# A two-block transformer kernel: each weight chunk's upper and lower part placed at one of sixteen offsets inside its buffer

## The chip, the cores and the metric

The kernel runs on one core of one Trainium2 chip. The metric is the device time of one execution in microseconds (us), the median of several runs. TensorE (PE in the profile) does the matrix products, VectorE (DVE), ScalarE (ACT) and GpSimd (POOL) the rest, and SyncE (SP) issues the loads of the weights.

## The reference

The reference is two model blocks of two layers each, at 256 tokens and a width of 1024. The first has a feed-forward part, a token mixer of three kinds of heads and a second feed-forward part in every layer; the second has a mixer of three other kinds and a feed-forward part with a convolution. Nearly all the arithmetic is in products of the tokens with large weight matrices:

```python
y = swiglu(modulate(x, ...), ffn_w13[l, 0], ffn_w2[l, 0])       # 1024 -> 2*2816 -> 1024
x = layer_norm(ALPHA * x + 0.5 * (1 + mod[:, 0, 2])[:, None, :] * y, ...)
y = token_mixer(modulate(x, ...), w_in[l], w_out[l], ...)
...
proj = x @ w_in                                                  # 1024 -> 4608, second block
u = depthwise_conv_centred(x @ w_up, conv_w, conv_b)             # 1024 -> 2*2816
ffn = (jax.nn.silu(gate) * val) @ w_down
```

## The kernel before

The weights come in 369 chunks of at most 128 partitions by 2048 float32 (8192 bytes a partition, 1 MB in all) in an order fixed beforehand (`SCHED`). 295 of them are matrices (`MATS`), numbered m from 0; the others feed a small sum on VectorE and play no part here. SyncE loads a chunk into one of four buffers `W`. ScalarE copies it, rounded to the reduced float32 of the PE array, into one of three buffers `H` (the upper part, line 586). VectorE subtracts that copy from `W` and writes the remainder into one of three buffers `L` (the lower part, line 601). Chunk m uses `H[m % 3]` and `L[m % 3]`. The tokens are held split in the same way (`XH` and `XL`, `hh` and `hl`, `mixh` and `mixl`, and `eh` and `el` for the first stage), and each product is made of three: upper by upper, lower by upper, upper by lower.

TensorE takes chunk m in one of these ways, each matmul with its own load of the stationary operand of 128 columns:

- `up` (lines 713 to 715): the stationary operand is a 128-column slice of `H` or `L`, the moving operand is 256 columns of `XH` or `XL`. In a chunk there are 2 tiles of 8 rows of 3 matmuls.
- `tokens` (742 to 744): the other way round, the stationary operand is of `XH` or `XL` and the moving one is 256 columns of `H` or `L`. In the first stage `eh` and `el` stand for `XH` and `XL` in both.
- `opening` (729 to 732): as `up`, in another order, for the first chunk of a stage.
- `down_bank` (757 to 759): the stationary operand is of `hh`/`hl` (feed-forward) or `mixh`/`mixl` (mixers), the moving one is 512 columns of `H` or `L`.

The order of the work is written out by program and is the same on every run. Semaphores tie it: ScalarE may write `H[m % 3]` when TensorE has done chunk m - 3 (`released`), VectorE waits for ScalarE, TensorE waits for VectorE (`lo_done`), and SyncE refills a `W` buffer when VectorE has read it.

Where the buffers lie follows from their sizes and the order in which they are allocated. In bytes of a partition: `H` at 68256, 76448 and 84640, `L` at 92832, 101024 and 109216, all of them 160 beyond a multiple of 512. `hh` and `hl` (117408, 139936), and `eh` and `el` (133792, 141984), are also 160 beyond a multiple of 512. `XH`, `XL`, `mixh` and `mixl` (from 200672 on) are 480 beyond one. Every slice that the matmuls take inside them starts a multiple of 512 bytes further on.

Of the kernel before, what the change touches and what calls it, by code (L numbers as in the profile page):

```python
# [9 lines left out]
F32R = mybir.dt.float32r  # L10
# [4 lines left out]
ADD, SUB, MUL, MAX, MIN = ALU.add, ALU.subtract, ALU.mult, ALU.max, ALU.min  # L15
# [7 lines left out]
CH = 2048  # L23
NW = 4
NH = 3
# [100 lines left out]
def width(c):  # L126
    return len(MIXCOLS[c[2]][1]) if c[0] == "win" else 256
# [189 lines left out]
def rr(ap, pattern, **k):  # L317
    return ap.rearrange(pattern, **k)
# [10 lines left out]
class Core:  # L329
# [22 lines left out]
    def keep(self, name, shape, dt=F32):  # L352
        t = self.place(name, shape, self.at, dt)
        self.at += self.size(shape)
        return t
# [11 lines left out]
    def buffers(self):  # L367
        keep = self.keep
        self.C = keep("cst", [128, NCONST])
        self.COL = keep("cols", [128, NROW])  # L370
        self.HD = keep("heads", [128, 4])
        self.CV = keep("cv", [128, 8])
        self.SC = keep("sc", [128, 8])
        self.POS = keep("pos", [128, 2], I32)
        self.CS = keep("cs", [128, 2, 2, 8])
        self.ones = keep("ones", [128, 128])
        self.AB = keep("ab", [128, 16])
        self.mod = [keep(f"mod{i}", [128, 3, 8]) for i in range(2)]
        self.X = keep("x", [128, 2, D])
        self.W = [keep(f"w{i}", [128, CH]) for i in range(NW)]  # L380
        self.H = [keep(f"h{i}", [128, CH], F32R) for i in range(NH)]
        self.L = [keep(f"l{i}", [128, CH], F32R) for i in range(NH)]
        x = self.top = self.top - 7 * 4096
        self.XH, self.XL = self.place("xh", [128, 8, T], x, F32R), self.place("xl", [128, 8, T], x + 8192, F32R)
        self.mixh1, self.mixl1 = self.place("mixh", [128, 8, T], x, F32R), self.place("mixl", [128, 8, T], x + 8192, F32R)
        g = self.gate_at = x + 16384
        self.G = self.place("gate", [128, D], g)
        self.acc = [self.place(f"acc{i}", [128, D], g + 4096 * i + 4096) for i in range(2)]
        self.GB2 = self.place("gb2", [128, 2, D], g + 4096)
        self.base = self.at  # L390
        self.ln_at = self.top - (8192 + 8192 + 2048 + 4096 + 128)
        ln = self.stack(self.ln_at, R=[128, 2, D], GB=[128, 2, D], tmp=[128, 2, 2, 128], tmp0=[128, 8, 128], st=[128, 2, 16])
        self.R, self.GB, self.tmp, self.tmp0, self.st = (ln[k] for k in ("R", "GB", "tmp", "tmp0", "st"))
        const = lambda k: self.C[:, CW[k][0]:CW[k][0] + CW[k][1]]
        self.ident, self.neg, self.causal, self.lvl, self.eye, self.both = (const(k) for k in ("ident", "neg", "causal", "lvl", "eye", "both"))
        self.ones64, self.rmask, self.freq, self.sgn, self.mhalf = (const(k) for k in ("ones64", "rmask", "freq", "sgn", "mhalf"))
        f = self.stack(self.base, hh=[128, NF, T], hl=[128, NF, T], sa=[128, 4, T], hf=[128, 2, T], yb=[128, 2, T])
        self.hh, self.hl, self.sa, self.hf, self.yb = (f[k] for k in ("hh", "hl", "sa", "hf", "yb"))
        assert f["end"] <= self.ln_at, (f["end"], self.ln_at)
        k = self.stack(self.base, memf=[128, 8, T], xf=[128, 8, T], eh=[128, 8, T], el=[128, 8, T], ftmp=[128, 8, T])  # L400
        self.memf, self.xf, self.eh, self.el, self.ftmp = (k[n] for n in ("memf", "xf", "eh", "el", "ftmp"))
        assert k["end"] <= self.ln_at
        k = self.stack(self.ln_at, mk0=[128, 4, T], mv0=[128, 2, 512], mk1=[128, 4, T], mv1=[128, 2, 512], z=[128, 2, 4, 8], p=[128, 2])
        self.kvb = [[k["mk0"], k["mv0"]], [k["mk1"], k["mv1"]]]
        self.rot_z, self.rot_p = k["z"], k["p"]
        assert k["end"] <= self.top
# [140 lines left out]

def made(m):  # L550

    return m + 2


class Feed:
# [5 lines left out]
    def load(self):  # L561
        k, e, n = self.k, self.e, self.n
        self.n += 1
        if n >= NW:
            o = n - NW
            if SCHED[o][0] == "ada":
                e.wait_ge(k.ada_sum, 2 * sum(c[0] == "ada" for c in SCHED[:o + 1]))
            else:
                e.wait_ge(k.lo_done, made(MATPOS.index(o)))
        z = 8 * width(SCHED[n])  # L570
        parts = [slice(0, 1024), slice(1024, CH)] if n == 0 else [slice(0, z)]
        for i, c in enumerate(parts):
            if n == 0:
                e.dma_start(k.memf[:, 4 * i:4 * i + 4, :], k.dram["memT"][:, 4 * i:4 * i + 4, :]).then_inc(k.d_mem[i], 16)
            e.dma_start(k.W[n % NW][:, c], k.dram["stream"][n][:, c]).then_inc(k.landed[n % NW] if n or i else k.d_first, 16)

    def hi(self, upto):

        k, e = self.k, self.e
        while self.m <= min(upto, len(MATS) - 1):  # L580
            m, n = self.m, MATPOS[self.m]
            z = 8 * width(MATS[m])
            e.wait_ge(k.landed[n % NW], 16 * (n // NW + 1))
            if m >= NH:
                e.wait_ge(*k.released(m - NH))
            e.copy(k.H[m % NH][:, 0:z], k.W[n % NW][:, 0:z]).then_inc(k.hi_done, 1)  # L586
            self.m += 1

    def lo(self, upto):

        k, e = self.k, self.e
        while self.n < len(SCHED) and (self.m <= upto or SCHED[self.n][0] == "ada"):
            n, c = self.n, SCHED[self.n]
            self.n += 1
            if c[0] == "ada":
                self.sum_ada(n, c)
                continue
            m, z = self.m, 8 * width(c)
            self.m += 1
            e.wait_ge(k.hi_done, made(m))  # L600
            e.tensor_tensor(k.L[m % NH][:, 0:z], k.W[n % NW][:, 0:z], k.H[m % NH][:, 0:z], SUB).then_inc(k.lo_done, 1)  # L601

    def sum_ada(self, n, c):
        k, e, v = self.k, self.e, self.a // 4
# [74 lines left out]
class Pe:  # L679
# [5 lines left out]
    def open(self):  # L685

        k, m = self.k, self.m
        self.m += 1
        self.p.wait_ge(k.lo_done, made(m) if m else 1)
        n = width(MATS[m])  # L690
        rows = 2 if MATS[m][0] in DOWN else 8
        v = lambda b: rr(b[:, 0:8 * n], "p (k n) -> p k n", k=rows)
        return v(k.H[m % NH]), v(k.L[m % NH])

    def bank(self):
        k, t = self.k, self.t
# [2700 lines left out]
```

## Time and profile before

| | |
|---|---|
| median of 3 runs | 2102.08 us (2100.36 to 2103.16) |
| span of the profiled execution | 2101.3 us |
| TensorE busy | 2002.5 us, 95% |
| weight loads of TensorE busy | 1854.1 us, 88% |
| VectorE busy | 1575.3 us, 75% |
| ScalarE busy | 1073.1 us, 51% |
| GpSimd busy | 308.4 us, 15% |
| granted TensorE clock, mean | 0.983 |

The profile gives the span of its execution, from the first to the last instruction, and no other time of it; the span is 0.8 us below the median of the runs. Matmuls are pipelined, so the duration of one (280 ns for one of 256 columns) is longer than the distance from its start to the next one's start. It is this distance, called the pace below, that times the work.

### The profile page before, as it was taken

The page shows a single profiled execution, that of the slowest core. Times are in us where ns is not written, and L with a number is a line of the kernel's source. Part 1 is how long each engine was busy: PE and PEld are TensorE (multiplying, and loading weights), DVE is VectorE, ACT ScalarE, POOL GpSimd, SP SyncE. Part 2 cuts the span into 40 slices and gives each one's busy share as a digit, 9 for nine tenths or more (in the row PEclk, how much of TensorE's full clock was granted, in tenths as well). Part 3 has the DMA queues.
Part 4 walks back from the last instruction along what each step waited for, and adds up shares of the span by engine and source line. Part 5 has one row for each costly group of instructions (what it writes and reads, how often), then busy time and mean ns, then how long its engine had stood idle before and what let it go on. Part 6 is the DMA issues. An engine that isn't in the chain of part 4 may idle for free.

```text
span 2101.3 us, 39270 instructions
## 1 busy us (share of the span) xinstructions
PE 2002.5 (95%) x16744; PEld 1854.1 (88%) x16744; DVE 1575.3 (75%) x2135; ACT 1073.1 (51%) x1516; POOL 308.4 (15%) x247
## 2 busy tenths in 40 slices
PE   7999989999999999899999999898999997989998
PEld 7999879979998998789889989887899887979996
DVE  6688788766987677688675649886788489758874
ACT  4543365455434443564554435565665375646652
POOL 0200032111000200203011004610120036002100
PEclk9999999999999999999999999899999999999999
DMA  9888743335985677443245663233465533324552
GB/s 378 325 315 330 279 161 132 106 120 203 354 340 205 243 284 303 148 163 122 82 173 207 252 226 118 101 141 115 147 202 193 205 125 141 122 101 161 202 199 80
DMA packets 60381, 409.85 MB, mean 195 GB/s; under 512 B 6896, under 2 KB 6896, under 8 KB 13872
## 3 DMA queue, kind: packets, MB, share of 16 engines
q1 hardware_dynamic: 54000, 384.85, 49.4%
q0 software_dynamic: 5920, 22.07, 3.1%
q8 instruction: 133, 2.18, 0.4%
q10 hardware_dynamic: 288, 0.42, 0.1%
q14 instruction: 40, 0.33, 0.0%
HBM read 404.17 MB, written 3.15 MB: 194 GB/s over the span
## 4 chain that ended last, share of the span: by engine, by line
PE 76%; DVE 14%; ACT 4%; POOL 2%; issue 2%; DMA 2%; SPq 0%; DVEq 0%; POOLq 0%; ACTq 0%
PE ps L713 13%; PE ps L714 13%; PE ps L715 13%; PE ps L757 7%; PE ps L759 6%; PE ps L758 6%; DVE l L601 4%; PE ps L742 2%; PE ps L1725 2%; PE ps L744 2%; PE ps L743 2%; DMA w<-in_stream 2%; PE ps L625 1%; DVE tmp L975 1%; ACT h L586 1%
## 5 line engine op out<-in xcount | busy, mean ns | idle before, releaser
L601 DVE TENSOR_TENSOR l<-w,h 128x2048 fp32r<-128x2048 f32 (+1 forms) x295 | 672.7, 2283 | 150.1 <-ACT h L586 149.7
L713 PE MATMUL ps<-xh,h 128*128 128x256 f32 x2544 | 722.3, 284 | 19.3 <-DVE gq L2423 9.4
L586 ACT CAST h<-w 128x2048 fp32r<-128x2048 f32 (+1 forms) x295 | 557.0, 1893 | 331.4 <-PE ps L759 162.1
L714 PE MATMUL ps<-xl,h 128*128 128x256 f32 x2544 | 713.6, 281 | 0.0
L715 PE MATMUL ps<-xh,l 128*128 128x256 f32 x2544 | 712.9, 280 | 0.0
L713 PEld LDWEIGHTS ps<-xh,h 128*128 128x128 f32 x2544 | 480.4, 189 | 27.6 <-DVE l L601 12.3
L714 PEld LDWEIGHTS ps<-xl,h 128*128 128x128 f32 x2544 | 480.3, 189 | 2.4 <-issue 2.4
L715 PEld LDWEIGHTS ps<-xh,l 128*128 128x128 f32 x2544 | 480.1, 189 | 0.0
L757 PE MATMUL ps<-h,hh 128*128 128x512 f32 x528 | 207.4, 393 | 0.0
L759 PE MATMUL ps<-h,hl 128*128 128x512 f32 x528 | 205.6, 389 | 0.0
L758 PE MATMUL ps<-l,hh 128*128 128x512 f32 x528 | 205.5, 389 | 0.0
L618 DVE SCALAR_TENSOR_TENSOR acc<-w,sc,acc 128x1024 f32<-128x1024 f32 x126 | 165.2, 1311 | 3.8 <-DMA w<-in_stream 1.1
L742 PE MATMUL ps<-h,xh 128*128 128x256 f32 (+1 forms) x512 | 150.8, 294 | 9.3 <-DVE l L601 9.3
L743 PE MATMUL ps<-l,xh 128*128 128x256 f32 (+1 forms) x512 | 145.6, 284 | 0.0
L744 PE MATMUL ps<-h,xl 128*128 128x256 f32 (+1 forms) x512 | 145.5, 284 | 0.0
L1021 POOL TENSOR_SCALAR st<-st 128x1 f32<-128x1 f32 x22 | 8.2, 374 | 814.8 <-DVE st L897 806.5
L759 PEld LDWEIGHTS ps<-h,hl 128*128 128x128 f32 x528 | 99.1, 188 | 20.8
L758 PEld LDWEIGHTS ps<-l,hh 128*128 128x128 f32 x528 | 99.2, 188 | 20.6 <-issue 0.5
L757 PEld LDWEIGHTS ps<-h,hh 128*128 128x128 f32 x528 | 99.1, 188 | 20.5 <-issue 0.5
L1254 DVE TENSOR_TENSOR hl<-hf,hh 128x256 fp32r<-128x256 f32 x132 | 55.6, 421 | 81.8 <-ACT hh L1249 81.1
L742 PEld LDWEIGHTS ps<-h,xh 128*128 128x128 f32 x512 | 100.1, 196 | 14.5 <-DVE l L601 10.3
L744 PEld LDWEIGHTS ps<-h,xl 128*128 128x128 f32 x512 | 100.3, 196 | 0.0
(425 smaller groups left out, 3007.1 us busy)
## 6 DMA issues: line engine op xcount, KB each, us to landing
w<-in_stream SPq DMA_DIRECT2D x361, 1024.0 KB, 4.9
GB<-in_vec POOLq DMA_DIRECT2D x20, 512.0 KB, 5.8
w<-in_stream SPq DMA_DIRECT2D x8, 512.0 KB, 4.1
gate<-in_vec POOLq DMA_DIRECT2D x6, 512.0 KB, 4.0
memf<-in_memT SPq DMA_DIRECT2D x2, 512.0 KB, 6.1
xf<-in_xT POOLq DMA_DIRECT2D x1, 1024.0 KB, 9.5
kv<-mk POOLq DMA_DIRECT2D x2, 512.0 KB, 6.1
kv<-mv POOLq DMA_DIRECT2D x2, 512.0 KB, 8.6
```

Of the source, the lines that this page charges most:

```text
L586: e.copy(k.H[m % NH][:, 0:z], k.W[n % NW][:, 0:z]).then_inc(k.hi_done, 1)
L601: e.tensor_tensor(k.L[m % NH][:, 0:z], k.W[n % NW][:, 0:z], k.H[m % NH][:, 0:z], SUB).then_inc(k.lo_done, 1)
L618: e.scalar_tensor_tensor(out=A[:, :], in0=W[:, i, :], scalar=k.SC[:, r:r + 1], in1=A[:, :], op0=MUL, op1=ADD).then_inc(k.ada_sum, 1)
L713: p.matmul(P[:, 0:T], H[:, r, o], xh[:, r, :], start=r == 0, stop=False)
L714: p.matmul(P[:, 0:T], H[:, r, o], xl[:, r, :], start=False, stop=False)
L715: i = p.matmul(P[:, 0:T], L[:, r, o], xh[:, r, :], start=False, stop=r == 7)
L742: p.matmul(P[:, 0:n], xh[:, r, o], H[:, r, :], start=r == 0, stop=False)
L743: p.matmul(P[:, 0:n], xh[:, r, o], L[:, r, :], start=False, stop=False)
L744: i = p.matmul(P[:, 0:n], xl[:, r, o], H[:, r, :], start=False, stop=r == 7)
L757: p.matmul(P[:, :], hh[:, f, o], H[:, i, s], start=b, stop=False)
L758: p.matmul(P[:, :], hh[:, f, o], L[:, i, s], start=False, stop=False)
L759: x = p.matmul(P[:, :], hl[:, f, o], H[:, i, s], start=False, stop=e)
```

## The change

`H` and `L` buffers grow by 128 elements (512 bytes a partition). A new function gives the place of chunk m: 8 elements (32 bytes) times m % 16 beyond the buffer's start. ScalarE's copy, VectorE's subtraction and TensorE's reads all use it.

```diff
-        self.H = [keep(f"h{i}", [128, CH], F32R) for i in range(NH)]
-        self.L = [keep(f"l{i}", [128, CH], F32R) for i in range(NH)]
+        self.H = [keep(f"h{i}", [128, CH + 128], F32R) for i in range(NH)]
+        self.L = [keep(f"l{i}", [128, CH + 128], F32R) for i in range(NH)]
...
+def place_in(b, m, z=CH, first=0):
+
+    o = 8 * (m % 16)
+    return b[m % NH][:, o + first:o + z]
...
-            e.copy(k.H[m % NH][:, 0:z], k.W[n % NW][:, 0:z]).then_inc(k.hi_done, 1)
+            e.copy(place_in(k.H, m, z), k.W[n % NW][:, 0:z]).then_inc(k.hi_done, 1)
...
-            e.tensor_tensor(k.L[m % NH][:, 0:z], k.W[n % NW][:, 0:z], k.H[m % NH][:, 0:z], SUB).then_inc(k.lo_done, 1)
+            e.tensor_tensor(place_in(k.L, m, z), k.W[n % NW][:, 0:z], place_in(k.H, m, z), SUB).then_inc(k.lo_done, 1)
...
-        v = lambda b: rr(b[:, 0:8 * n], "p (k n) -> p k n", k=rows)
-        return v(k.H[m % NH]), v(k.L[m % NH])
+        v = lambda b: rr(place_in(b, m, 8 * n), "p (k n) -> p k n", k=rows)
+        return v(k.H), v(k.L)
```

Chunk 0, which is written by two lines of its own, has the offset 0 in both kernels. No instruction is added, removed or moved on any of the five engines: the two programs are the same row by row, apart from addresses. `H` now starts at 68256, 76960 and 85664 and `L` at 94368, 103072 and 111776, still 160 beyond a multiple of 512, and chunk m lies 32 * (m % 16) bytes beyond that. What is allocated behind the six buffers (`hh`, `hl`, `eh`, `el` among it) moves up by 3072 bytes, which is a multiple of 512; `XH`, `XL`, `mixh` and `mixl` are counted from the top of the memory and stay.

## Rows read from the trace of the kernel before

**Rows 1.** The page: the span, and each engine's busy time.

```profile
span 2101.3 us, 39270 instructions
PE 2002.5 (95%) x16744; PEld 1854.1 (88%) x16744; DVE 1575.3 (75%) x2135; ACT 1073.1 (51%) x1516; POOL 308.4 (15%) x247
```

**Rows 2.** The page: the chain that ended last, shares by engine.

```profile
PE 76%; DVE 14%; ACT 4%; POOL 2%; issue 2%; DMA 2%; SPq 0%; DVEq 0%; POOLq 0%; ACTq 0%
```

**Rows 3.** Stretches of feed-forward work: busy us, granted clock, DMA share, GB/s.

```profile
680.00:800.00 120.00, 119.50 (x1004) 118.35 (x1004) 84.61 (x84) 54.83 (x65) 12.01 (x6) 1.00 0.71 268
1210.00:1270.00 60.00, 60.00 (x289) 50.36 (x288) 32.51 (x29) 16.89 (x9) 3.73 (x8) 1.00 0.58 208
```

**Rows 4.** Groups by form: busy us, mean ns; then idle time before.

```profile
L713 PE MATMUL ps<-xh,h 128*128 128x256 f32 x2544 | 722.3, 284 | 19.3 <-DVE gq L2423 9.4 <-DVE l L601 6.4 <-ACT K L3214 3.4
L601 DVE TENSOR_TENSOR l<-w,h 128x2048 fp32r<-128x2048 f32 x289 | 665.4, 2305 | 142.7 <-ACT h L586 142.5
L586 ACT CAST h<-w 128x2048 fp32r<-128x2048 f32 x289 | 550.7, 1910 | 321.8 <-PE ps L759 152.5 <-PE ps L715 77.7 <-DMA w<-in_stream 67.1
L757 PE MATMUL ps<-h,hh 128*128 128x512 f32 x528 | 207.4, 393 | 0.0
L742 PE MATMUL ps<-h,xh 128*128 128x256 f32 x480 | 141.8, 295 | 9.3 <-DVE l L601 9.3
L757 PE MATMUL ps<-h,mixh 128*128 128x512 f32 x160 | 69.4, 434 | 0.6
L729 PE MATMUL ps<-xh,h 128*128 128x256 f32 x144 | 41.8, 329 | 1.1 <-ACT mv L1091 0.7 <-DVE xl L1108 0.3
L713 PE MATMUL ps<-eh,h 128*128 128x256 f32 x64 | 19.5, 305 | 11.0 <-DVE l L1125 10.0 <-DVE l L601 0.9
```

**Rows 5.** Timeline, `up` in a feed-forward stage: start us, us; 51 starts apart.

```profile
699.86 0.28 PE L713 MATMUL ps<-xh,h 128*128 128x256 f32 x1
...
705.87 0.28 PE L713 MATMUL ps<-xh,h 128*128 128x256 f32 x1
```

**Rows 6.** Timeline, `up` late in the second mixer: 21 starts apart.

```profile
1428.66 0.28 PE L713 MATMUL ps<-xh,h 128*128 128x256 f32 x1
...
1431.04 0.28 PE L713 MATMUL ps<-xh,h 128*128 128x256 f32 x1
```

**Rows 7.** Timeline, `tokens` in the first stage: 42 starts apart.

```profile
61.52 0.28 PE L744 MATMUL ps<-h,el 128*128 128x256 f32 x1
...
66.56 0.28 PE L744 MATMUL ps<-h,el 128*128 128x256 f32 x1
```

**Rows 8.** Timeline, `tokens` in the second mixer: 39 starts apart.

```profile
1386.00 0.28 PE L742 MATMUL ps<-h,xh 128*128 128x256 f32 x1
...
1390.59 0.28 PE L742 MATMUL ps<-h,xh 128*128 128x256 f32 x1
```

**Rows 9.** Timeline, `down_bank` with `hh`: 96 starts apart.

```profile
1217.84 0.39 PE L757 MATMUL ps<-h,hh 128*128 128x512 f32 x1
...
1239.60 0.39 PE L757 MATMUL ps<-h,hh 128*128 128x512 f32 x1
```

**Rows 10.** Timeline, `down_bank` with `mixh`: 33 starts apart.

```profile
441.97 0.39 PE L757 MATMUL ps<-h,mixh 128*128 128x512 f32 x1
...
449.67 0.39 PE L757 MATMUL ps<-h,mixh 128*128 128x512 f32 x1
```

**Rows 11.** Waits, the largest of the weight chunks: us, times, longest us.

```profile
ACT h L586 <- PE ps L759: 162.1, 47, 5.5
DVE l L601 <- ACT h L586: 149.7, 74, 4.4
PE ps L742 <- DVE l L601: 12.4, 6, 3.6
```

## The prediction

> **What bounds the kernel now.** I read the page first. TensorE is busy for 2002.5 of the 2101.3 us [rows 1], and it holds 76% of the chain that ended last [rows 2]. Then I cut out stretches of the feed-forward stages with the view by windows. There TensorE has no gaps: 119.5 of 120 us and 60.0 of 60, at the full clock, while VectorE is busy for 84.6 of the 120 and the DMA engines are at 71% and 58% [rows 3]. The waits say the same from the other side. ScalarE waits 162 us in total for TensorE to give `H` back, and the costliest wait of TensorE for the lower part is 12.4 us [rows 11]. So the time of most stages is a count of matmuls times their pace, and the feeding engines have slack.
>
> The pace is what the change can touch, so I measured it in the timeline as the distance between two starts divided by their count. The reader should see that it isn't one number. I give it beside 106.7 and 213.3 ns, which are 256 and 512 columns at one per cycle of 2.4 GHz.
>
> - `up` in the feed-forward stages: 6.01 us for 51, so 117.8 ns [rows 5]. The same instruction late in the second mixer: 2.38 us for 21, so 113.3 ns [rows 6].
> - `tokens` with `eh`: 5.04 us for 42, so 120.0 ns [rows 7]. `tokens` with `xh`: 4.59 us for 39, so 117.7 ns [rows 8]; in most other places of the mixers its starts stand, by the timeline, as in [rows 6].
> - `down_bank` with `hh`: 21.76 us for 96, so 226.7 ns [rows 9]. With `mixh`: 7.70 us for 33, so 233.3 ns [rows 10].
>
> Two things follow. The same instruction with the same places relative to 512 bytes can run at 117.8 or 113.3 ns, so there are states that it falls into and keeps. And the partner counts: `eh` and `hh` lie 160 beyond a multiple of 512 like `H`, `xh` and `mixh` lie 480 beyond one, and with equal places 256 columns are slowest (120.0) while 512 columns are fastest (226.7). Apart from the addresses I find no difference between the `tokens` of [rows 7] and those of [rows 8]. That is an argument, not proof, that the relative place of the stationary and the moving operand sets part of the pace.
>
> **The change part by part.** No instruction is added, removed or moved. So every term is a count times a change of duration.
>
> ScalarE's copy and VectorE's subtraction: 1910 and 2305 ns [rows 4]. `W`, `H` and `L` all lie at 160 beyond a multiple of 512 today, which would be the worst case if their places could collide, and I take nothing from them and add nothing. If the copy grew by 5% (0.1 us of a chunk's 5.7 us, 48 matmuls by 117.8), the slack of the feeding engines would hide it [rows 3, 11]. The DMAs into `W` and their addresses don't change. The shift of the buffers behind by 3072 bytes keeps every place relative to 512. I cost both at nothing; TensorE's own work covers them, and bare they would be worth 0.1 us in a chunk.
>
> The matmuls: the relative place now goes through sixteen values, 32 bytes apart, one for each chunk. Only two of the sixteen relations (equal, and 320 bytes apart in one sense or the other) are seen in this trace, so each term is bounded by the lowest and the highest pace seen of the same shape: 113.3 to 120.0 ns for 256 columns and 226.7 to 233.3 for 512. The counts are three times those of [rows 4].
>
> - `up` with `xh`, 7632 at 117.8. The state was kept through whole stages while all chunks had one place. With a new place at each chunk I expect it to be drawn anew every 5.7 us. I take the lower state for half of the chunks and the middle of the two upper values, 118.9, for the other half: 116.1 ns, so 7632 x 1.7 = 13.0 us less. Bounds: 34 us less (all at 113.3) to 17 us more (all at 120.0).
> - `down_bank` with `hh`, 1584 at 226.7, the lowest seen. Half of the chunks at 233.3: 1584 x 3.3 = 5.3 us more. Bounds: 0 to 10.6 us more.
> - `tokens` with `xh` and `opening`, 1440 and 432, now between 113.3 and 117.8. From the middle, 115.6, to 116.1: 1.0 us more. Bounds: 4 us less to 8 us more.
> - `down_bank` with `mixh`, 480 at 233.3: half of the chunks at 226.7, 1.6 us less. Bounds: 3.2 us less to 0.
> - The first stage with `eh`, 384 at 120.0 to 116.1: 1.5 us less, of which some vanishes, since the stage also waits for its loads. Bounds: 2.6 us less to 0.
>
> Sum: -13.0 + 5.3 + 1.0 - 1.6 - 1.5 = -9.8 us. On the span of 2101.3 that gives 2091.5, and on the median, 0.8 us higher, 2092.3. I say 2092. The sum of the bounds is 44 us less to 36 us more, where all terms would have to end on one side.
>
> What a rule says against it: the Trainium skill (SBUF — State Buffer, Who interferes with whom) gives TensorE two independent read ports, one for the moving operand and one for the weights, and says that PE and ACT never wait on anyone. By it the sum would be zero and the time 2102. The rows above don't decide it, but 120.0 against 113.3 ns for the same shape is something that this rule alone doesn't explain.
>
> **The rivals.**
>
> *Places don't matter (2102).* The states come from how the queue of TensorE filled, and `eh` differs from `xh` by something else of its stage. For it: `up` has both 117.8 and 113.3 at the same places [rows 5, 6], so something other than the place sets at least that difference. Against it: 120.0 in the first stage and nowhere else, 226.7 with `hh` and 233.3 with `mixh` [rows 7, 9, 10]. Chance 0.28. Close to it is that the places matter and the terms cancel, 2098 to 2106: 0.07.
>
> *Only the place of the moving operand matters, and today's is a bad one (2082).* All operands of the reduced kind start 32 bytes beyond a multiple of 64 (160 and 480 both do). If a start on a multiple of 64 saved a matmul the sixteenth by which 226.7 and 113.3 exceed the bare columns, half of the chunks would gain where `H` and `L` are moving: 1584 x 13.3 / 2 = 10.6 us with `hh`, 3.2 with `mixh`, and 1440 x 6.7 / 2 = 4.8 in `tokens`. That is 18.6 us, so 2083. `up` would stay, as its moving operand is `xh`. For it: the excess of the lowest pace seen is exactly a sixteenth of the columns for both sizes. Against it: nothing in the trace starts elsewhere, so nothing shows a gain. Chance 0.12.
>
> The Trainium skill (TensorE: Matmul & The Clock Gate, Back-to-back issue gap) gives for a single isolated matmul N / 2.4 + 2.5 ns, which would be 109.2 and 215.7 ns here. By an estimate from it, all of `up` and of `down_bank` at those paces would take 7632 x 8.6 + 1584 x 11.0 + 480 x 17.6 = 91 us off; no run here shows these paces for this kind of operand.
>
> *The equal place was the good one for 512 columns, and the stationary operand's place is indifferent (slower, 2112).* Then `up`, in which `H` is stationary, keeps 117.8 ns, and `down_bank` with `hh` loses 226.7 in fifteen of sixteen chunks: 1584 x 15/16 x 6.7 = 9.9 us more. It decides once more than about half of the chunks of `hh` lose their pace and `up` gains less than 0.7 ns. For it: 226.7 with `hh` against 233.3 with `mixh`. Against it: the first stage has 120.0 ns in `up` and in `tokens` alike, so the roles seem not to matter. If `up` also went to 118.9 it would be 2120. Chance 0.23 for this side.
>
> The forecast itself, faster by some 5 to 25 us through `up`, has 0.30.
>
> **How the numbers follow.** Faster: the forecast and the aligned start, 0.42. Same: 0.35, from no effect and from terms that cancel. Slower: 0.23. I take 0.2%, 4.2 us, as what a measurement of this kernel tells from no change; its three runs lie 2.8 us apart. The predicted time is that of the likeliest single case. The range reaches from `up` going two thirds of the way to 113.3 (23 us) with some of the gain of aligned starts on top, 2070, to the slower rival with a part of its worse form, 2116. Outside I leave 0.1 on each side. Within the likeliest case alone it is 2077 to 2098.
>
> **What would show it.** In the changed kernel's timeline the pace of `up` should differ from chunk to chunk, repeat after sixteen chunks, and lie at 117.8 ns in a part of them only; `down_bank` with `hh` should have 226.7 ns in some chunks and more in others. The copy and the subtraction should keep 1910 and 2305 ns, and the granted clock its level. If the paces are those of [rows 5, 9] in all chunks, places don't matter. If `down_bank` falls below 226.7 in every second chunk, it is the aligned start. The forecast is wrong if `up` stays at 117.8 in nearly all chunks, or goes to 120 as often as to 113.3, or if VectorE or a load becomes what TensorE waits for in the stages in which the pace falls. The weakest step is the share of chunks given to each pace; no row shows it.

## The result and the profile after

The changed kernel takes 2114.73 us (median of 3 runs, 2114.09 to 2118.04) against 2102.08 before: 1.0065 times as long, 95% interval 1.0045 to 1.0085. The prediction said 2092 and faster; it is slower by about 12.7 us, the side of its third rival, which had 2112. The ratios here and below stand with their 95% intervals; they differ by up to 0.13% from the quotient of the two medians. Each experiment has its own executions of the kernel before beside it, and its ratio is against these.

The page of the changed kernel, span and busy times:

```profile
span 2111.9 us, 39270 instructions
PE 2015.4 (95%) x16744; PEld 1860.8 (88%) x16744; DVE 1576.4 (75%) x2135; ACT 1071.8 (51%) x1516; POOL 307.9 (15%) x247
```

Its groups by form, for the lines that were 713, 601, 586, 757, 742 and 729 before (all lines have moved down by 6):

```profile
L719 PE MATMUL ps<-xh,h 128*128 128x256 f32 x2544 | 727.0, 286 | 17.4 <-DVE gq L2429 8.2 <-DVE l L607 5.6 <-ACT K L3220 3.5
L607 DVE TENSOR_TENSOR l<-w,h 128x2048 fp32r<-128x2048 f32 x289 | 665.1, 2304 | 149.7 <-ACT h L592 149.6
L592 ACT CAST h<-w 128x2048 fp32r<-128x2048 f32 x289 | 549.8, 1907 | 334.1 <-PE ps L765 164.8 <-PE ps L721 76.6 <-DMA w<-in_stream 68.7
L763 PE MATMUL ps<-h,hh 128*128 128x512 f32 x528 | 209.9, 398 | 0.0
L748 PE MATMUL ps<-h,xh 128*128 128x256 f32 x480 | 141.6, 295 | 9.9 <-DVE l L607 9.8
L763 PE MATMUL ps<-h,mixh 128*128 128x512 f32 x160 | 69.0, 431 | 0.2
```

The copy and the subtraction have their durations of before, 1907 and 2304 ns against 1910 and 2305 [rows 4], so the places cost ScalarE and VectorE nothing. TensorE is busy 13 us longer, and the span is 10.6 us longer. TensorE's idle time before line 719 is 17.4 us, 19.3 before [rows 4], so no feeding engine has become what it waits for. ScalarE waits 334 us ahead of its copies, 322 before, and most of it for TensorE.

Where TensorE lost it shows in the timeline of the changed kernel. Four rows of `up`, for chunks 266 and 268, with 45 starts between the first and the last of each pair, and four of `down_bank` with `hh`, for chunks 285 and 288, 21 starts apart:

```profile
1934.34 0.29 PE L721 MATMUL ps<-xh,l 128*128 128x256 f32 x1
...
1939.74 0.28 PE L721 MATMUL ps<-xh,l 128*128 128x256 f32 x1
...
1945.78 0.28 PE L721 MATMUL ps<-xh,l 128*128 128x256 f32 x1
...
1950.88 0.28 PE L721 MATMUL ps<-xh,l 128*128 128x256 f32 x1
...
2042.53 0.40 PE L765 MATMUL ps<-h,hl 128*128 128x512 f32 x1
...
2047.45 0.40 PE L765 MATMUL ps<-h,hl 128*128 128x512 f32 x1
...
2059.35 0.39 PE L765 MATMUL ps<-h,hl 128*128 128x512 f32 x1
...
2064.12 0.39 PE L765 MATMUL ps<-h,hl 128*128 128x512 f32 x1
```

Chunk 266 (m % 8 = 2) runs at 5.40 us / 45 = 120.0 ns, chunk 268 (m % 8 = 4) at 113.3; before, both ran at 117.8, the pace of [rows 5]. Chunk 268 isn't typical of its place: 5 of the 19 chunks with m % 8 = 4 run below 114 ns, and most at 117.8. Chunk 285 (m % 8 = 5) runs at 4.92 us / 21 = 234.3 ns and chunk 288 (m % 8 = 0) at 227.1, against 226.7 before [rows 9]. The durations of single instructions hardly show it (398 against 393 ns); the distance between the starts does.

Taken over all chunks, with the starts of the matmuls sorted by the chunk that they read, the mean pace in ns by m % 8 is this (m and m + 8 agree within 0.5 ns in `up`, and within 1 ns in `down_bank`; gaps between starts that are waits are left out, and so are the two chunks of `tokens` with 128 columns). By the kernel's own tables there are 368 chunks, 296 of them matrices, one fewer and one more than said at the start; of `up` with `xh` there are 160, of `down_bank` with `hh` 66, of `tokens` with `xh` and 256 columns 30. Before, their means are 117.7, 226.9 and 114.8 ns; in the changed kernel they are 118.3, 232.4 and 118.0.

```
m % 8          0     1     2     3     4     5     6     7
up           117.4 117.7 119.8 118.3 116.6 118.0 118.6 119.8
down, hh     228.0 233.5 229.4 233.7 232.6 234.0 233.1 232.9
tokens       115.3 118.1 119.7 117.4 117.0 119.8 118.5 117.9
```

And the time of the stages in the profiled executions, in us, as the differences between the first starts of stages. The six feed-forward stages are split into `up` and `down`; the last three columns belong to runs told of below:

```
                          before   changed   e7_place_by_kind   e9_kind_lower_0   e10_sweep_down_only
six up parts               767.5      +2.2              -13.9             -22.3                 -16.4
six down parts, hh         409.2      +7.8                0.0               0.0                  +7.8
four mixers, up, tokens    676.3      +2.1               +2.9              +0.3                  +0.2
four mixers, down          172.0      -1.5               -1.2              -1.1                  -1.2
first stage                 57.5      -0.2               -1.9              -1.9                  -1.6
```

So three quarters of the change's cost is in `down_bank` with `hh`. The paces of `tokens` rose by some 3 ns on 1440 matmuls, 4 us if all of it counted, but the mixers got only 2.1 us longer. What the mixers say is weak, though, since their time moves by itself: in e2 below, whose paces are those of before, the same four parts take 9.0 us more than before. The first mixer's `up` and `tokens` part takes 171.4 us in the kernel before and 175.0 in e2, for the same 2057 matmuls (these rows have the stretch, the busy us of each engine, the granted clock, the DMA share and GB/s):

```profile
266.20:437.60 171.40, 159.43 (x2057) 147.93 (x2057) 134.44 (x244) 95.28 (x157) 34.28 (x26) 0.98 0.37 132
266.30:441.30 175.00, 161.34 (x2057) 149.98 (x2057) 135.48 (x244) 95.43 (x157) 33.37 (x26) 0.96 0.36 130
```

The granted clock is 0.98 in the first and 0.96 in the second. So the 2.1 us of the mixers can't be put down to the change. The `down` parts with `hh` are the steady ones: their total is the same within 0.1 us in before, e1, e2, e7 and e9.

### The profile page after: what moved, and what is told of

It is laid out like the page before. It is cut to its first block, busy times and chain, and to the rows that moved or that the text cites. A ratio compares the mean times of both kernels' runs of the same rounds, so it can differ in the third digit from the quotient of the medians.

```text
span 2111.9 us, 39270 instructions
## 1 busy us (share of the span) xinstructions
PE 2015.4 (95%) x16744; PEld 1860.8 (88%) x16744; DVE 1576.4 (75%) x2135; ACT 1071.8 (51%) x1516; POOL 307.9 (15%) x247
## 4 chain that ended last, share of the span: by engine, by line
PE 75%; DVE 14%; ACT 4%; DMA 2%; issue 2%; POOL 2%; SPq 0%; DVEq 0%; POOLq 0%; ACTq 0%
PE ps L719 13%; PE ps L721 13%; PE ps L720 13%; PE ps L763 7%; PE ps L764 7%; PE ps L765 7%; DVE l L607 4%; DMA w<-in_stream 2%; PE ps L1731 2%; PE ps L748 2%; PE ps L750 2%; PE ps L749 2%; PE ps L631 1%; DVE tmp L981 1%; ACT h L592 1%
## 5 line engine op out<-in xcount | busy, mean ns | idle before, releaser
L719 PE MATMUL ps<-xh,h 128*128 128x256 f32 x2544 | 727.0, 286 | 17.4 <-DVE gq L2429 8.2
L749 PEld LDWEIGHTS ps<-l,xh 128*128 128x128 f32 x512 | 99.1, 193 | 0.0
```

What stands on the lines that cost most here:

```text
L719: p.matmul(P[:, 0:T], H[:, r, o], xh[:, r, :], start=r == 0, stop=False)
L749: p.matmul(P[:, 0:n], xh[:, r, o], L[:, r, :], start=False, stop=False)
```

## The experiments

The theory after the result (A): the distance, modulo 256 bytes, between the places of the two operands in their partition sets the pace of the reduced-float32 matmuls. The rivals are: larger buffers or the shift of what lies behind them (B); that the place changes at all between chunks (C); the own place of `H` and `L`, whatever their partner (D). All kernels below are edits of the changed kernel unless said otherwise.

**e1_grown_buffers and e2_step_256.** The larger buffers alone, and two places 256 bytes apart:

```diff
-    o = 8 * (m % 16)
+    o = 0                 # e1
+    o = 64 * (m % 2)      # e2
```

> The changed kernel with the offset 0 for every chunk: only the six buffers are 512 bytes larger, and what lies behind them is 3072 bytes further on. If the relative place of the two operands within 256 bytes sets the pace (theory A), the paces are those of before, 117.8 ns in the feed-forward up and 226.7 in down_bank with hh, and the time is 2102, within 0.2% of before. If the shift of the other buffers or the larger buffers cost the time (theory B), it is near 2114.

> Offset 256 bytes for odd chunks, 0 for even ones: the place changes from chunk to chunk, the place within 256 bytes doesn't. Theory A: 2102, within 0.2% of before, with 226.7 ns in all down_bank chunks with hh. Theory C (that the place changes at all between chunks costs time, by breaking a state or by the address arithmetic): up to all of the 12 us of the change, 2108 to 2114, with down_bank above 226.7 in most chunks.

Measured: 2107.15 us, 1.0015 times before (1.0000 to 1.0030), and 2104.89 us, 1.0009 times (0.9996 to 1.0022). The mean paces are those of before, 226.9 and 227.0 ns in `down_bank` with `hh` and 117.8 and 117.7 in `up` and `opening`. Rows of e2 for the odd chunk 291, 21 starts apart, in the timeline:

```profile
2074.14 0.39 PE L765 MATMUL ps<-h,hl 128*128 128x512 f32 x1
...
2078.90 0.39 PE L765 MATMUL ps<-h,hl 128*128 128x512 f32 x1
```

That is 226.7 ns, at a place 256 bytes from that of the chunk before. B and C fall by the paces, and the period of 256 bytes stands, which makes eight places of the sixteen. The times lie a little high; the intervals leave at most 0.3% for anything besides the places.

**e3_all_64.** One place for all, 64 bytes on (`o = 16`, and the two lines that write chunk 0 follow it).

> One offset of 64 bytes for all chunks. Theory A takes the paces of the chunks with m % 8 = 2 of the changed kernel for all: up 119.8 (7632 x 2.0 = 15 us more), down_bank with hh 229 (4 us more), tokens 119.6 (7 us more), with mixh 228 (2.5 us less), together some 25 us more than before, 2127. Theory C (change between chunks) has no change here and expects 2102; so does theory B.

Measured: 2124.77 us, 1.0106 times before (1.0092 to 1.0120). Its timeline has, for chunk 266 and 45 starts,

```profile
1944.95 0.28 PE L721 MATMUL ps<-xh,l 128*128 128x256 f32 x1
...
1950.36 0.28 PE L721 MATMUL ps<-xh,l 128*128 128x256 f32 x1
...
2082.08 0.39 PE L765 MATMUL ps<-h,hl 128*128 128x512 f32 x1
...
2086.88 0.39 PE L765 MATMUL ps<-h,hl 128*128 128x512 f32 x1
```

120.2 ns, and 228.6 ns for chunk 290 and 21 starts. The chunk paces of the changed kernel carry over to a kernel in which nothing varies. Theory C, which had 2102, falls once more. The sum, some 25 us more, was 3 to 4 us too high: the kernel before took 2103.36 us beside this run, so the median rose by 21.4.

**e4_partners_64.** The kernel before, with `H` and `L` untouched and their partners moved:

```diff
-        x = self.top = self.top - 7 * 4096
+        x = self.top = self.top - 7 * 4096 - 64
...
-        self.base = self.at
+        self.base = self.at + 64
```

> The kernel before with H and L where they were, and the partners moved: XH, XL, mixh, mixl 64 bytes down, hh, hl, eh, el 64 bytes up. Theory A (only the distance counts): up as in the chunks with m % 8 = 2, 119.8; tokens 119.6; down_bank with hh as with m % 8 = 6, 233.2 (10 us more); with mixh 228; together 30 us more, 2132. Theory D (the own place of H and L counts, whatever their partner): all paces as before, 2102.

Measured: 2132.43 us, 1.0139 times before (1.0122 to 1.0157). In `down_bank` with `hh`, 21 starts apart:

```profile
2090.66 0.39 PE L759 MATMUL ps<-h,hl 128*128 128x512 f32 x1
...
2095.56 0.40 PE L759 MATMUL ps<-h,hl 128*128 128x512 f32 x1
```

That is 233.3 ns; the mean in `up` and `opening` is 120.0. D falls: `H` and `L` never moved. This is the run that shows a relation between the operands. It also fits e3 pace by pace. In both, `H` and `L` come out level, within 256 bytes, with `XH`, `XL`, `mixh` and `mixl`, and the means are equal within 0.3 ns: 119.9 in `up` and 119.7 in `tokens` in both, 228.0 and 228.3 in `down_bank` with `mixh`. With `hh` the places part, `H` 64 bytes ahead in e3 and 64 bytes behind in e4, and there e3 has 228.8 and e4 233.4.

**e5_lower_pair_64.** The kernel before, with all lower parts 64 bytes on, `L` and its partners together (`XL`, `mixl`, `hl` and `el` get 64 bytes of room ahead of them, `qT` and `aT` behind them too).

> The kernel before with all lower parts 64 bytes on: L and their partners XL, mixl, hl, el together; the upper parts stay. Theory A1 (what counts is the distance between the moving operand of a matmul and the stationary operand that is loaded for the next one while it streams): in the fixed order of three matmuls these two are always both upper or both lower parts, so no distance changes and the time is 2102. Theory A2 (the distance of the two operands of the same matmul counts): two of each three matmuls get a new distance, up about 118.8, down_bank with hh 229.7, tokens 117, together some 15 us more, 2117.

Measured: 2111.94 us, 1.0041 times before (1.0026 to 1.0057). `down_bank` with `hh`, 21 starts:

```profile
2069.89 0.39 PE L760 MATMUL ps<-h,hl 128*128 128x512 f32 x1
...
2074.74 0.39 PE L760 MATMUL ps<-h,hl 128*128 128x512 f32 x1
```

231.0 ns, mean 231.4, where A1 had 226.7 and A2 229.7; `tokens` rose to 118.5, where A2 had 117; `up` stayed at 117.8, where A2 had 118.8. A1 falls, since it allowed no change. A2 has the sign in two of the three uses and none of the sizes: neither pairwise rule is enough.

**e6_step_16.** 16 bytes in place of 32 (`o = 4 * (m % 16)`).

> The changed kernel with 16 bytes in place of 32 between the sixteen places. Theory A: the even places repeat the first eight steps of the changed kernel (down_bank with hh 226.7 at 0, 228.9 at 64 bytes, some 233 elsewhere; up 119.8 at 64 and at 224 bytes), and if the odd ones lie between their neighbours the time is that of the changed kernel, 2115. If the unit is 32 bytes, an odd place has the pace of the even one below it, and the time is the same. A place that is a multiple of 16 and not of 32 with a pace below 113.3 or 226.7 would be news.

Measured: 2110.35 us, 1.0037 times before (1.0023 to 1.0050). The 16-byte places are places of their own: in `down_bank` with `hh`, 227.6 ns at 240 bytes and 231.4 at 16. None is below the lowest of before. At 128 bytes, `up` has 113.5 ns, where the changed kernel has 116.6 at the same place. So the place doesn't determine the pace alone. The expectation that an odd place copies or averages its neighbours was wrong, and the time came out near the expected 2115 without it.

**e7_place_by_kind.** Each chunk gets the place that suits its use, with the 32-byte steps UP = 4, TK = DN = 0, MX = 2, EU = 2, ET = 6, and 0 for the opening chunks (`STARTS`):

```diff
+def step_of(m):
+    c = MATS[m]
+    if m in STARTS:
+        return 0
+    if c[0] in ("w2", "wdn"):
+        return DN
+    if c[0] in ("wout", "wout2"):
+        return MX
+    if c[0] in ("w13", "wup"):
+        return UP
...
-    o = 8 * (m % 16)
+    o = 8 * step_of(m)
```

> Each chunk's place by how TensorE uses it, from the paces of the changed kernel: 128 bytes where H is stationary against XH (up), 0 for down_bank with hh, for tokens and for the opening chunks, 64 for down_bank with mixh, 64 and 192 in the first stage. Theory A: up at 116.6 as in the chunks with m % 8 = 4 (9 us less; 34 us less if the lower state at 113.3 lasts, nothing if the upper one at 117.7 does), with mixh 228.3 (2.5 us less), down_bank with hh unchanged, in all 2090 (2066 to 2100). Theory C (a change of place between chunks costs): above 2102.

Measured: 2089.60 us, 0.9933 times before (0.9913 to 0.9953), faster than both kernels. In the timeline nearly every chunk of `up` is in one of two states, at the same places: of the 126 in the feed-forward stages 84 run near 113.3 ns and the others near 117.8. They come in runs of 2 to 21 chunks, and one of the six `up` parts keeps the lower pace throughout. `down_bank` with `mixh` fell to some 228 ns in the mean.

**e8_lower_swept.** As e7, but `L` at 32 x (m % 8) bytes: `o = 8 * (m % 8)` for `L`.

> As the place by kind, but L at 32 x (m % 8) bytes with H where the kind puts it: a map of the pace over the place of L alone. If only the distance to the partner counts, L is one stream of three, so up lies within 113.3 to 120.0 and moves by about a third of what moving both did; down_bank with hh lies between 226.7 and 229 in all chunks. If the distance between H and L counts too, paces outside of these appear. Time 2100 to 2112.

Measured: one run, 2113.48 us. With `L` alone moved by 64 bytes, `down_bank` with `hh` has 231.7 ns in place of 226.7, more than the 228.8 that moving both has (e3), and `up` goes beyond all that was seen, here 45 starts of chunk 266:

```profile
1934.38 0.28 PE L743 MATMUL ps<-xh,l 128*128 128x256 f32 x1
...
1939.88 0.28 PE L743 MATMUL ps<-xh,l 128*128 128x256 f32 x1
```

122.2 ns. So something beyond each operand's distance to its own partner counts, and theory A in its narrow form is not complete. The distance between `H` and `L` is the nearest candidate; no run separates it from the order in which the three matmuls follow each other. The map also has a find: with `H` at 128 and `L` at 0, all 22 chunks of `up` run at 113.3 to 114.7.

**e9_kind_lower_0.** e7 with that pair of places in `up`:

```diff
-    o = 8 * step_of(m)
+    lower = b[0].name[0] == "l"
+    o = 0 if lower and step_of(m) == UP else 8 * step_of(m)
```

> The place by kind, but in up only H lies at 128 bytes and L at 0, as in the chunks with m % 8 = 0 of the run with L swept, where up ran at 113.3 to 114.5 in all 22 chunks. Theory E (a pair of places for H and L decides whether up can fall into the upper state at 117.8): up at 113.5 in nearly all chunks, where the place by kind has 115.0 with 6 to 8 of some 20 chunks at 117.8; 7632 x 1.5 = 11 us less than the place by kind, 2078. If the state comes from what ran before and not from the places, the mixture stays and the time is 2090.

Measured: 2078.10 us, 0.9872 times before (0.9851 to 0.9893), the fastest kernel of this study. 44 starts of `up` in its timeline:

```profile
1902.51 0.28 PE L744 MATMUL ps<-xh,l 128*128 128x256 f32 x1
...
1907.50 0.28 PE L743 MATMUL ps<-xl,h 128*128 128x256 f32 x1
```

113.4 ns, and of the 160 chunks of `up` in the profiled execution none is in the upper state; the highest has 115.7 ns in the mean. The time is the expected 2078, and the rival by which the mixture stays (2090) falls.

**e10_sweep_down_only.** The sixteen places for `w2` and `wdn` chunks only, 0 for all others.

> The sixteen places only for the chunks of down_bank with hh, 0 for all others. Theory A: these five stages take the 7.8 us more that they take in the changed kernel, the rest is as before, so 8 us above before, 2111. If the stages act on each other through states or buffers, more or less than that. If the slower half of the change were in up, this would be within 0.2% of before.

Measured: 2109.06 us, 1.0028 times before (1.0005 to 1.0051). The stage table above has the same 7.8 us in the down parts as the changed kernel (there are six of them, not five). The profiled execution is not the median one: its span is 2090.3 us, since three of its six `up` parts ran in the lower state throughout and a fourth for the most part, at the very places of the kernel before. 45 starts of `up`, then 21 of `down_bank` at m % 8 = 3:

```profile
1917.26 0.28 PE L721 MATMUL ps<-xh,l 128*128 128x256 f32 x1
...
1922.36 0.28 PE L721 MATMUL ps<-xh,l 128*128 128x256 f32 x1
...
2054.25 0.40 PE L765 MATMUL ps<-h,hl 128*128 128x512 f32 x1
...
2059.16 0.39 PE L765 MATMUL ps<-h,hl 128*128 128x512 f32 x1
```

113.3 and 233.8 ns. A whole `up` part at 113.3 is 4.5 us shorter, and these parts together make up the 16.4 us of the table. The time of this kernel spreads from 2092 to 2118 us and that of the kernel before, in the runs beside it, from 2090 to 2109. The states account for the lower end, at which the profile was taken; that they account for the rest is not shown, and 2118 is more than all chunks at 117.8 would give (the expected 2111). The mixers, which in e2 took 9.0 us more at unchanged paces, are a second source.

**e11_all_on_64.** The kernel before with every operand of these matmuls on a multiple of 64 and all distances kept (`self.at += 32` ahead of `H`, and `self.top` 480 lower).

> The kernel before with H, L and all their partners 32 bytes on (XH, XL, mixh, mixl 480 down, which is 32 up within 256), so that they start on multiples of 64, and all distances stay. Theory A: every pace as before, 2102, within 0.3%. The rival of the prediction by which a start on a multiple of 64 saves a sixteenth: 226.7 becomes 213 to 220 in down_bank and 113.3 becomes 107 to 110, 10 to 40 us less.

Measured: 2101.51 us, 1.0002 times before (0.9982 to 1.0021). `down_bank` with `hh`, 21 starts:

```profile
2057.68 0.39 PE L760 MATMUL ps<-h,hl 128*128 128x512 f32 x1
...
2062.44 0.39 PE L760 MATMUL ps<-h,hl 128*128 128x512 f32 x1
```

226.7 ns, as before. A start on a multiple of 64 saves nothing, and the excess of a sixteenth stays. Here too one of the six `up` parts ran at 113.3 throughout, 121.8 us in place of 126.3.

**e12_upper_swept.** As e9, with `H` at 32 x (m % 8) bytes in `up`.

> As the place by kind with L at 0, but H at 32 x (m % 8) bytes in up: a map over the place of H alone. Two of the three streams of up use H. Theory A: 117.8 at 0, 113.3 at 128, the worst, 120 or above, where H is 64 bytes on and so equal to XH; no pace below 113.3. A pace below 113.3 would be a better place than any found. Time near 2100.

Measured: one run, 2096.41 us. `up` has 117.8 ns at 0, 113.4 in most chunks at 128, 115.6 in most at 192, and means between 117.8 and 118.7 elsewhere. The worst was not 64 bytes (117.9) but 32 (118.7): with `L` at 0, an upper part level with `XH` no longer costs what it costs when both are (119.9 in e3). No pace lies below 113.3.

## Why the prediction was wrong, step by step

**The time** of 2114.73 us lies inside the range of 2070 to 2116, but only because the range reached to the slower rival. The forecast itself, faster through `up`, had the wrong sign.

**The bound** was right: TensorE's pace is the time, and nothing that feeds it took over. In e9 the feed-forward stages got 22 us shorter and the whole kernel 24.

**That the relative place sets part of the pace** was right, argued from two relations only. e4 shows it with `H` and `L` untouched and removes the rival "places don't matter"; e11 removes "an aligned start". The rule of the Trainium skill (SBUF — State Buffer, Who interferes with whom), two independent read ports and a TensorE that never waits on anyone, would have given 2102 for every one of these kernels; e3 and e4 measured 2125 and 2132, so here the measurement decides. The rule may hold between engines, for which no run here shows a cost; between the reads of TensorE itself it doesn't describe these times. That the reads collide is only argued from a distance that matters; no run shows a port.

**The term for `up`, "the lower state for half of the chunks", -13.0 us, is the step that failed.** It came out at +2.2 us in the six feed-forward parts, and over all 160 chunks the mean rose from 117.7 to 118.3 ns where the prediction had 116.1. The prediction took the two paces seen at one distance (113.3 and 117.8) for draws that a new place at each chunk would make anew. The changed kernel shows no lower state at the places other than 0 and 128 bytes: their chunks run at 116.7 to 120.1 ns, chunk after chunk. It appeared in 5 of 19 chunks at 128 bytes and in 1 of 22 at 0, so in 6 of 160 and not in half of them. The 42 chunks at 64 and 224 bytes ran near 119.8, a sign that the prediction had named as showing it wrong. And even where the lower state exists, it isn't drawn anew for each chunk: e7 has it in runs of 2 to 21 chunks, and e10 keeps it through three whole stages.

**The term for `down_bank` with `hh`, +5.3 us, was too small by a third**: 7.8. The step behind it was "half of the chunks at 233.3"; it was six of the eight places at 232.6 to 234.0, and 229.4 at 64 bytes. e10 puts these 7.8 us in these chunks alone.

**The smaller terms**: `tokens` and `opening` at +1.0: their paces rose by some 3 ns in place of 0.5, about 6 us if all of it counted. Part of the error is the start: the pace of `tokens` before was 114.8, not the 115.6 taken as the middle. The time of the mixers, +2.1 us, can't decide it, as e2 shows. `mixh` at -1.6, measured -1.5. The first stage at -1.5, measured -0.2. Copy and subtraction at 0: 0, by their durations. The shifted buffers at 0: e1 has the paces of before and leaves at most 0.3%.

**The slower rival** had the right chunks: `down_bank` loses its good distance, 7.8 us where it had 9.9, and `up` doesn't gain. That its 2112 lies within 3 us of the result is in part luck, for its reason, that the stationary operand's place is indifferent, is wrong: in e3 `up` rises from 117.8 to 120.0, where `H` is stationary.

**What stays open**: what makes the three-matmul sequence at 113.3, 115.6, 117.8, 120.0 or 122.2 ns. The distance to the partner enters (e3, e4), and something beyond it, perhaps the distance between `H` and `L` (e5, e8, e12). Where two states are possible, no run shows what decides between them; that it is what ran before is only a guess. That the spread between runs of one kernel comes from these states is shown for two profiled executions (e10, and e11 by one part) and argued for the rest.

## What to carry to other kernels

Where a kernel is bound by back-to-back matmuls, measure the distance between starts in the timeline, not the duration of one, and do it stage by stage: a few per cent in it is the whole kernel's few per cent, and here it depended on where the operands lay relative to each other within 256 bytes. A sweep over places by chunk number costs time as a kernel but is a cheap map; put the best place of each use into the next kernel, and sweep the operands one at a time, as the best pair (upper part 128 bytes on, lower part at 0) wasn't on the diagonal. A mean over two values seen at one setting is no forecast for settings that haven't been seen.

## What the hardware showed unexpectedly

- The pace of these reduced-float32 matmuls depends on the distance between the places of the two operands, with a period of 256 bytes (e4, e2), and on more than that (e8): 113.3 to 122.2 ns for 256 columns, 226.7 to 234.3 for 512. A step of 16 bytes already matters (e6: 227.6 ns at 240 bytes, 231.4 at 16).
- With both parts level with their partners, 512 moving columns have their best pace (226.7 with `hh`, 228.0 in e3 with `mixh`) and 256 columns nearly their worst (120.0 in the first stage, 119.9 in e3). With `H` level and `L` not, 256 columns have 117.9 (e12).
- The same instructions at the same places have two lasting paces, 117.8 and 113.3 ns: in e10 five of the six `up` parts keep one of them for all their 121 to 132 us. A pair of places at which only the lower one was seen (e9) made the kernel 1.3% faster than before.
- In none of the 14 kernels does a chunk of 256 or 512 columns have a mean pace below 113.3 or 226.6 ns. That is 17/16 of the 106.7 and 213.3 ns that the prediction sets beside them.
